# Weighted values with the head's values stationary and the turned probabilities moving, and the shares applied before the turn

## The reference, cut to what matters

```python
p = jax.nn.softmax(s, axis=-1)                       # first block, 8 heads
o = jnp.einsum('btngk,btknd->btngd', p, v_g)         # weighted values

p = jnp.exp(scores - m[..., None])                   # second block, kind 0
den = jnp.sum(p, axis=-1)
o = jnp.einsum('brnqhk,brnkhd->brnqhd', p, vb) / den[..., None]
ya = ya * jax.nn.silu(za)                            # the gate, per token and feature
pa = ya @ w_proj_a
```

## Time and profile before

| | |
|---|---|
| runs | 1718.6 us median of 3 (1718.58 to 1718.79) |
| the profiled execution's own time | 1716.0 us |
| its span, first to last instruction | 1714.1 us |
| TensorE busy | 1688.9 us, 13056 matmuls |
| VectorE busy | 1169.4 us |
| ScalarE busy | 941.9 us |
| GpSimd busy | 191.8 us |

### The profile page before, as it was taken

One profiled execution on the slowest core, in us unless ns is written; L12 is line 12 of the kernel. 1 busy time (PEld: TensorE's weight loads), 2 busy tenths in 40 slices (PEclk: granted clock), 3 DMA queues, 4 the chain that ended last, 5 costly groups with the idle time before them and its releaser, 6 DMA issues.

```text
span 1714.1 us, 30930 instructions
## 1 busy us (share of the span) xinstructions
PE 1688.9 (99%) x13056; PEld 1539.5 (90%) x13056; DVE 1169.4 (68%) x1631; ACT 941.9 (55%) x1386; POOL 191.8 (11%) x208
## 2 busy tenths in 40 slices
PE   7999999999999999999999999999999999999998
PEld 6989999999998989999999998888788988887887
DVE  7877555787877976547787875656765656567664
ACT  5584434654455574335554554665774546657742
POOL 0454500000001645200000000000000100000000
PEclk9999999999999999999999999999999999999999
DMA  6433523445444423424455545434345453344451
GB/s 227 170 133 106 182 103 124 172 174 195 173 170 170 173 99 131 161 100 153 168 196 183 179 182 177 148 124 172 133 156 188 163 200 145 126 169 148 150 194 49
DMA packets 48056, 268.33 MB, mean 157 GB/s; under 512 B 13552, under 2 KB 14448, under 8 KB 16176
## 3 DMA queue, kind: packets, MB, share of 16 engines
q1 hardware_dynamic: 38448, 264.80, 43.4%
q10 hardware_dynamic: 8704, 0.53, 0.3%
q0 software_dynamic: 768, 1.05, 0.3%
HBM read 264.52 MB, written 1.84 MB: 155 GB/s over the span
## 4 chain that ended last, share of the span: by engine, by line
PE 91%; DVE 5%; ACT 1%; POOL 1%; issue 0%; DMA 0%; SPq 0%; POOLq 0%; DVEq 0%; ACTq 0%
PE bank L1389 15%; PE bank L1390 14%; PE bank L1391 14%; PE bank L2484 10%; PE bank L2486 10%; PE bank L2485 10%; DVE w_low L905 2%; PE bank L2514 1%; PE bank L1626 1%; PE bank L1628 1%; PE bank L1627 1%; PE bank L2555 1%; PE bank L2502 1%; PE bank L1783 1%; DVE arena L1131 1%; ACT arena L632 1%
## 5 line engine op out<-in xcount | busy, mean ns | idle before, releaser
L905 DVE TENSOR_TENSOR w_low<-slab,w_high 128x2048 fp32r<-128x2048 f32 x250 | 585.8, 2348 | 237.3 <-ACT w_high L566 230.5
L1389 PE MATMUL bank<-act_high,w_high 128*128 128x256 f32 x2304 | 660.4, 287 | 0.1
L1390 PE MATMUL bank<-act_low,w_high 128*128 128x256 f32 x2304 | 651.8, 283 | 0.0
L1391 PE MATMUL bank<-act_high,w_low 128*128 128x256 f32 x2304 | 651.6, 283 | 0.0
L566 ACT ACTIVATE w_high<-slab 128x2048 fp32r<-128x2048 f32 x250 | 474.0, 1897 | 154.9 <-PE bank L2486 88.4
L1389 PEld LDWEIGHTS bank<-act_high,w_high 128*128 128x128 f32 x2304 | 441.7, 192 | 9.0 <-issue 6.1
L1390 PEld LDWEIGHTS bank<-act_low,w_high 128*128 128x128 f32 x2304 | 441.9, 192 | 1.1 <-issue 1.0
L1391 PEld LDWEIGHTS bank<-act_high,w_low 128*128 128x128 f32 x2304 | 441.8, 192 | 0.0
L2484 PE MATMUL bank<-w_high,act_high 128*128 128x512 f32 x768 | 305.8, 398 | 0.0
L2486 PE MATMUL bank<-w_low,act_high 128*128 128x512 f32 x768 | 300.7, 392 | 0.0
L2485 PE MATMUL bank<-w_high,act_low 128*128 128x512 f32 x768 | 299.9, 390 | 0.0
(11 more groups left out here) (240 smaller groups left out, 1732.6 us busy)
## 6 DMA issues: line engine op xcount, KB each, us to landing
slab<-stream_a SPq DMA_DIRECT2D x144, 1024.0 KB, 4.8
slab<-stream_b SPq DMA_DIRECT2D x104, 1024.0 KB, 4.7
residual<-x_t SPq DMA_DIRECT2D x4, 256.0 KB, 5.5
lora_weights<-lora SPq DMA_DIRECT2D x2, 512.0 KB, 8.0
out_t<-residual SPq DMA_DIRECT2D x4, 256.0 KB, 2.2
d_inverse<-arena POOLq DMA_DIRECT2D x2, 256.0 KB, 2.4
constants<-common SPq DMA_DIRECT2D x1, 384.0 KB, 9.6
constants_a<-const_a SPq DMA_DIRECT2D x1, 368.0 KB, 10.0
```

Source lines behind the costliest of these rows:

```text
L905: line.did(line.eng.tensor_tensor(core.wl[u % PARTS][:, 0:SLAB_WIDTH[u]], core.slab[u % SLABS][:, 0:SLAB_WIDTH[u]], core.wh[u % PARTS][:, ...
L1389: eng.matmul(out, wh, xh, start=first, stop=False, skip_group_check=True)
L1390: eng.matmul(out, wh, xl, start=False, stop=False, skip_group_check=True)
L1391: return eng.matmul(out, wl, xh, start=False, stop=last, skip_group_check=True)
```

## The change

The two operands of the weighted values change places. Now one head's values (128 keys x 64 features) are stationary and its turned probabilities move. For the first 128 keys both query blocks move in one product of 256 columns; for the second 128 keys only the second query block does, 128 columns. A pair takes four products instead of six, and the outputs have the features on the partitions: head 0 of the pair on partitions 0 to 63, head 1 on 64 to 127, 256 tokens in the columns. Since a token's denominator is then no longer a per-partition factor, the shares are applied before the turn: VectorE multiplies the exponentials by the reciprocals in place (`dve_share`: `share` in the a stages, `combine` for k < 8 in the b stages), and the turn waits for it (`shared`, `combined`) instead of for the exponentials.

In the a stages the output needs no transposes any more: pv on ScalarE and VectorE writes the high and low halves from bank 7 for each pair, and post is gone. In the b stages ScalarE copies bank 7 into the arena for each pair (VectorE's part of pv is gone), and the gate z is transposed instead of the gated output: z_turn(i) and y(i) behind the units (V, 2), (V, 3), (Q, 0), (Q, 1), and post(i), now from the arena, one unit later. The branch product in the a stages waits for one pair's halves at a time. The late turn goes from pair 0 of kind 0 to head 8, the first of kind 1.

```diff
+def dve_share(core, line, k, buf, tally):
+    rden = core.small[:, RDEN_:RDEN_ + 4]
+    line.settled()
+    line.did(line.eng.reciprocal(rden, core.small[:, DEN_ + 4 * (k % 4):][:, 0:4]))
+    line.settled()
+    for m in range(2):
+        part = buf[:, :, SPAN[m]]
+        line.did(line.eng.tensor_tensor(part, part, rden[:, 2 * m:2 * m + 2].unsqueeze(2).broadcast_to([P, 2, WIDTH[m]]), ALU.mult),
+                 tally if m else None)
+
+def pe_weighted(eng, out, p_t, value):
+    blocks = p_t.rearrange("p (n t) -> p n t", t=P)
+    for s in range(2):
+        for p in range(2):
+            o, v = out[HD * p:HD * p + HD], value(s, p)
+            if s == 0:
+                ins = eng.matmul(o[:, 0:T].rearrange("p (m t) -> p m t", m=2), v, blocks[:, p:2 * p + 3:2 + p], start=True, stop=False,
+                                 skip_group_check=True)
+            else:
+                ins = eng.matmul(o[:, P:T], v, blocks[:, 3 + 2 * p], start=False, stop=True, skip_group_check=True)
+    return ins
...
@@ schedule_a @@
-        work = [... (("pv", 3), ("turn", 2), ("scores", 0)) ...]
+        work = [... (("pv", 3), ("turn", 2), ("share", 1), ("scores", 0)) ...]
-    put(("ga", 1), ("invert", 0), ("tok", 1), ("post", 0), ("post", 1))
+    put(("ga", 1), ("invert", 0), ("tok", 1))
@@ schedule_b @@
-            late = (kind, n) == (0, 2)
+            late = (kind, n) == (1, 2)
-                put(UNITS_B[host + n], ("turn_late", 0))
+                put(UNITS_B[host + n], ("turn_late", 8))
-    put(("V", 3), ("y", 0), ("y", 1), ("y", 2), ("y", 3))
-    for i, unit in enumerate((("Q", 0), ("Q", 1), ("K", 0), ("K", 1))):
-        put(unit, ("post", i))
+    for i, unit in enumerate((("V", 2), ("V", 3), ("Q", 0), ("Q", 1), ("K", 0))):
+        if i < 4:
+            put(unit, ("z_turn", i), ("y", i))
+        if i:
+            put(unit, ("post", i - 1))
@@ a, ScalarE and VectorE: pv @@
+        act(core.xh[:, k, :], bank[7][:, 0:T], ACT.Copy, sem("ya_high"))
+        did(tt(core.xl[:, k, :], bank[7][:, 0:T], core.xh[:, k, :].bitcast(F32), ALU.subtract), sem("dve_emptied7"))
@@ b, ScalarE: pv, k < 8 @@
+            act(core.a(BO_ + k)[:, 0], bank[7][:, 0:T], ACT.Copy, sem("act_emptied7"))
@@ b, VectorE: pv gone; y and post, kind 0 @@
+            o = core.a(BO_ + 2 * i, 2)
+            did(tt(o, heads(bank[6 + i % 2], T), o, ALU.mult), sem(f"dve_emptied{6 + i % 2}"))
+            did(tt(low, core.a(BO_ + 2 * i, 2), high, ALU.subtract), sem("y_low"))
@@ b, TensorE: turn, pv, z_turn @@
+        sem("combined").at_least(eng, k + 1)
-            banks.fill(7, "dve")
+            banks.fill(7, "act")
+            ins = pe_weighted(eng, bank[7], p_t, lambda t, p: v[:, t, P * i + HD * p:P * i + HD * p + HD])
+    def z_turn(i):
+        if i == 0:
+            eng.wait_ge(*sem("z_ready").upto(1))
+        b = 6 + i % 2
+        banks.fill(b, "dve")
+        ... four transposes of by_token(core, BZ_[0], m), as post had of the output
```

More of the change, by code:

```diff
@@ L421, in schedule_a @@
         put(unit, *([("conv", n - 2)] if 2 <= n < 6 else []), *rwkv[n])
-        work = [(name, n - lag) for name, lag in (("pv", 3), ("turn", 2), ("scores", 0)) if 0 <= n - lag < 4]
+        work = [(name, n - lag) for name, lag in (("pv", 3), ("turn", 2), ("share", 1), ("scores", 0)) if 0 <= n - lag < 4]
         put(unit, *(work + [ROUND_NEXT] if unit == ("uc", 2) else [ROUND_NEXT] + work))
@@ L767, in turn, with pv @@
             act(turned_of(core, k, APT_)[:, at:at + n], bank[b][:, 0:n], ACT.Copy, sem(f"act_emptied{b}"))
-    def post(n):
-        eng.wait_ge(*sem("outputs_turned").next(eng))
-        act(core.xh[:, 2 * n:2 * n + 2, :], heads(bank[6 + n], T), ACT.Copy, sem("ya_high"))
+    def pv(k):
+        eng.wait_ge(*sem("weighted").upto(k + 1))
+        act(core.xh[:, k, :], bank[7][:, 0:T], ACT.Copy, sem("ya_high"))
     def lora_inputs(_):
@@ L1152, in scores, with share @@
         did(ts(mx, mx, -1.0, None, ALU.mult), sem("maxed"))
+    def share(k):
+        eng.wait_ge(*sem("exps").upto(k + 1))
+        dve_share(core, line, k, scores_of(core, k, ASC_), sem("shared"))
     def pv(k):
[L1155 to L1166, removed]
         eng.wait_ge(*sem("ya_high").next(eng))
-        did(tt(core.xl[:, 2 * n:2 * n + 2, :], heads(bank[b], T), core.xh[:, 2 * n:2 * n + 2, :].bitcast(F32), ALU.subtract),
-            sem(f"dve_emptied{b}"))
+        did(tt(core.xl[:, k, :], bank[7][:, 0:T], core.xh[:, k, :].bitcast(F32), ALU.subtract), sem("dve_emptied7"))
         line.tell(sem("ya_done"))
@@ L1564, in tile @@
         def tile(i, k):
-            if i == 0 and k % 2 == 0:
+            if i == 0 and name == "ya_done":
+                eng.wait_ge(*sem(name).upto(k + 1))
+            elif i == 0 and k % 2 == 0:
                 eng.wait_ge(*sem(name).upto(k // 2 + 1))
@@ L1684, in turn @@
         buf = scores_of(core, k, ASC_)
-        eng.wait_ge(*sem("exps").upto(k + 1))
+        eng.wait_ge(*sem("shared").upto(k + 1))
         for m, b in enumerate((6, 5)):
@@ L1697, in pv @@
         eng.wait_ge(sem("act_emptied5").sem, turn.at[k])
-        p_t = turned_of(core, k, APT_)
         banks.fill(7, "dve")
[L1700 to L1716, removed]
-                                    core.const("ident"))
-        ins.then_inc(sem("outputs_turned").sem, 1)
+        pe_weighted(eng, bank[7], turned_of(core, k, APT_),
+                    lambda t, p: half_of(core, WS_, t)[:, P + HD * p:P + HD * p + HD]).then_inc(sem("weighted").sem, 1)
     def lora(_):
@@ L2218, in post @@
         kind, i = n // 4, n % 4
-        eng.wait_ge(*sem("outputs_turned").next(eng))
         at = 8 * (1 - kind) + 2 * i
-        scale = core.small[:, LAM_ + 1:LAM_ + 2] if kind else 1.0
-        act(core.xh[:, at:at + 2, :], heads(bank[6 + i % 2], T), ACT.Copy, sem("y_high"), scale=scale)
+        if kind:
+            eng.wait_ge(*sem("outputs_turned").upto(n + 1))
+            act(core.xh[:, at:at + 2, :], heads(bank[6 + i % 2], T), ACT.Copy, sem("y_high"), scale=core.small[:, LAM_ + 1:LAM_ + 2])
+        else:
+            eng.wait_ge(*sem("outputs_gated").upto(n + 1))
+            act(core.xh[:, at:at + 2, :], core.a(BO_ + 2 * i, 2), ACT.Copy, sem("y_high"))
     def gate(g):
@@ L2354, in combine @@
     def combine(k):
+        eng.wait_ge(*sem("exps").upto(k + 1))
         if k < 8:
+            dve_share(core, line, k, scores_of(core, k, BSC_), sem("combined"))
             return
-        eng.wait_ge(*sem("exps").upto(k + 1))
         rden = shares(k)
@@ L2385, in y @@
         kind, i = n // 4, n % 4
+        if kind == 0:
+            eng.wait_ge(*sem("outputs_turned").upto(n + 1))
+            if n == 0:
+                eng.wait_ge(*sem("act_emptied7").upto(16))
+            o = core.a(BO_ + 2 * i, 2)
+            did(tt(o, heads(bank[6 + i % 2], T), o, ALU.mult), sem(f"dve_emptied{6 + i % 2}"))
+            line.tell(sem("outputs_gated"))
+            return
         if i == 0:
-            eng.wait_ge(*sem("z_ready").next(eng))
+            eng.wait_ge(*sem("z_ready").upto(2))
         if n == 4:
@@ L2409, in post @@
                     op1=ALU.subtract), sem(f"dve_emptied{b}"))
+            line.tell(sem("y_low"))
         else:
-            did(tt(low, heads(bank[b], T), high, ALU.subtract), sem(f"dve_emptied{b}"))
-        line.tell(sem("y_low"))
+            did(tt(low, core.a(BO_ + 2 * i, 2), high, ALU.subtract), sem("y_low"))
     def merge(i):
```

62 lines of the change are left out of this document (24 added, 38 removed).

## The result

The changed kernel takes 1728.1 us (median of 8 runs, 1723.6 to 1731.3), the kernel before 1718.6 (8 runs, 1716.5 to 1719.3): a ratio of 1.0055, 95% interval 1.0041 to 1.0068. That is 9.5 us slower, where 3.7 us faster was forecast and 1721.5 was the top of the range. The profiled execution took 1729.8 us for a span of 1728.0, at a mean granted clock of 0.987 of 2.4 GHz (before: 0.993).

A forecast was written before the change was run, and what follows sets the result against it. TensorE's own queue was taken as the bound, plus places where it waits for late engines. Terms of -2.1 (b steps and qk_turn), -0.7 (b turn order) and -0.9 (a stages) made -3.7 us, hence 1714.9 us, range 1711.3 to 1721.5.

The forecast's parts named there:

- The step: One weighted-value step on TensorE: 0.85 plus 0.09 to 0.19 us against 1.29, taken as 0.30 us saved.
- Rivals 3 and 4: Weighted-value step: 3, half overlap, saves nothing, 1718.6 us, chance 0.13; 4, no overlap, 1722.2 to 1723.8 us, chance 0.17.
- Waits of the b stages: b stages: TensorE waits for ScalarE's bank 7 copy in six places, 0.3 to 0.5 us each; such hosts lose 0.15.
- two new waits of 0.75: In each b stage TensorE waits 0.75 us for head 0's shares (`combined`) before its turn.
- none at head 8: b stages: with turn(8) put last, the 1.1 us wait before its transposes (L2524) is covered.
- The a stages' line: a stages: scores(1) and pair 1's maxima 2.2 to 3.2 us later, L1748 1.1 us late; net -0.9 us for both.
- a wait of TensorE elsewhere: Sign of being wrong: TensorE waits at places not named, such as the gate's transposes for `z_ready`.
- later than 103.68: a stages: GpSimd's L1949 comes later than 103.68 us, so ScalarE's square starts 0.6 to 1.6 us later.
- rival 2: a stages: full overlap, GpSimd and VectorE miss each other, 1.1 us back in each: 1712.0 us, chance 0.2.
- The 2 us to spare before the first chunk: a stages: after the attention part, the orders before the first chunk have over 2 us to spare.
- the transposes: a stages: the attention output's eight transposes go, 0.95 us net a stage, 1.9 us over two stages.

The follow-up runs named there:

- b_one_half: Against b_only, both heads' weighted-value products on the same column half, the second head's outputs left out: 1721.5 us, ratio 1.0026.
- b_only: Against the changed kernel, the a stages' programs and order of work put back as before, b stages as changed: 1715.6 us, ratio 0.9993.
- low_last: Against the changed kernel, VectorE's low half of the a stages' weighted values moved to the end of its host: 1725.2 us, ratio 1.0035.
- first_share_last: Against the changed kernel, only in the second host VectorE does scores(1) ahead of share(0): 1722.9 us, ratio 1.0021.
- mended: Against the changed kernel, a-stage scores ahead of the previous pair's shares, VectorE copy of bank 7, pair 2's turn last for both softmaxes: 1713.0 us, ratio 0.9981.
- a_no_share: Against the changed kernel, the a stages' shares (reciprocal and products) left out, hand-overs kept: 1716.2 us, ratio 0.9993.

## Why the prediction was wrong

- **The step.** Forecast 0.85 us or more with a cost of 0.09 to 0.19 for the change of form, so 0.30 saved; measured 0.81 us, a little under the 0.85 to 0.95 named, and 0.35 us saved a host. Right, at the upper edge of its bounds. b_one_half shows the cause, overlap. The Trainium skill ("TensorE: Matmul & The Clock Gate", packing small matmuls) would have a load overlap only where row groups differ; here all 128 rows are shared and 0.81 against 1.45 us says otherwise, as its table does, which has 2.38 times for three column tiles. Rivals 3 and 4 fall.
- **Waits of the b stages.** Forecast: hosts with a raw copy 0.15 longer, two new waits of 0.75, none at head 8. Measured: 0.16 longer (9.04 against 8.88), 0.65, none. For both stages -2.8 was forecast and -3.0 (0.3) measured at full clock. The waits for the ScalarE copy are 2.9 us, six of 0.5, where six of 0.3 to 0.5 were forecast; they eat what the larger saving brings.
- **The a stages' line: the step that failed.** It stood at -0.9 for both stages, with 1.1 us of lateness a stage, 1.8 at most, at L1748. Against b_only the changed a stages cost 7.6 us at full clock and 3.9 more through the clock (0.9910 to 0.9888). The prediction named a wait of TensorE elsewhere as a sign of being wrong: L1741, L1732 and L1828 are three. Five things were off.
  - The maxima of pair 1 came 4.2 us late (97.64 to 101.89), not 2.2 to 3.2. The delay by share(0) was foreseen, and is 2.8 us (scores(1) at 98.08 for 95.26), 1.7 of it collision. Not foreseen was that the delay carries the tiny negation behind it onto GpSimd's next operation, 1.4 us more. The trace of before had a sign of that, as the negation of pair 0 meets a GpSimd operation there:

```profile
91.64 1.29 POOL L1943 TENSOR_TENSOR arena<-arena 128x512 f32<-128x512 f32 x1
...
91.70 1.27 DVE L1152 TENSOR_SCALAR small<-small 128x4 f32<-128x4 f32 x1
```

  - GpSimd was forecast to be done with the keys later than 103.68, as before. It was early: the multiplication starts at 99.94 for 101.78, as its collision with the split went away (1.42 us for 3.09), which rival 2 had thought possible. It gave nothing back, since ScalarE now waited for the maxima.
  - The prediction followed this delay to L1691 and L1748 and not to bank 5, which passes from the copy of the turned probabilities to the sums of kk. That wait had no row before, since the copy came in time: 4.3 us in both stages.
  - VectorE's own wait for ScalarE's high half was in no term of the sum. pv was costed on ScalarE's queue alone; but what stands behind it on VectorE (a share, the scores) waits too. low_last measures it at 3.5 us.
  - The clock was taken as given. The three profiled kernels with waits of over 1.5 us at L1741 or L1732 (changed, low_last, first_share_last) have seven of them; five were followed within 2 us by 3 to 7 us at 1.2 GHz, two weren't (that at 617.19 above is one). Their mean clocks are 0.9888, 0.9881 and 0.9886 against 0.9907 to 0.9917 in the other sets of the changed forms, with standard errors of 0.0003 to 0.0009. A stretch of lower clock at 128 to 136 us comes in b_only's profile too, with no such wait, so single dips prove nothing; the means do show the difference. What decides whether a wait is followed by one stays open.
- **The 2 us to spare before the first chunk, and the transposes.** The 2 us aren't there: L1828 waits 1.5 us a stage for the inverses even in mended. The shares aren't the cause, as a_no_share waits 1.45 and 1.42 us there. Nor was there room before: TensorE came to this product 43.7 us after the last product of the chunks (159.91 to 203.65, start to start) without a wait, and in a_no_share, without the eight transposes between, it is there after 43.0 us and the inverses after 44.45 (161.75, 206.20). So most of the 1.9 us booked for the transposes turned into waiting here. Why the inverses also land later was not separated.

## What to carry to other kernels

Where work is put ahead of the link that others wait for, follow that link through every bank and every queue it feeds until the slack is used, including hand-overs that show no wait yet; and look at what tiny instruction lands beside a long GpSimd operation. When waits of a few kernels are compared, take the span times the granted clock beside the median. A regrouping of matmuls can be right and be lost by where its helpers stand: kept out of the a stages, with one copy on another engine and one more turn put last, the kernel is 0.6% faster than before (8.1 us at full clock, 2.4 of them from the turn order alone).

## What the runs showed of the hardware

- Products of 128 rows by 64 columns on the two column halves of TensorE run side by side in fp32, 0.81 against 1.45 us for eight records, in either order of the program.
- A VectorE tensor_scalar on 128x4 elements took 0.17 us alone, 0.30 to 0.65 in part and 1.74 us in full collision with a GpSimd tensor op of 1.90 us. The Trainium skill ("SBUF — State Buffer", on the shared port pair) names the lock; the trace agrees: the op of 1.74 us ends at 101.86, GpSimd's at 101.84, and the one of 1.27 us at 92.97, GpSimd's at 92.93. So the price was what the GpSimd operation had left, however small the VectorE op.
- Five of seven waits of TensorE of 1.55 to 2.19 us in the attention hosts were followed by 3 to 7 us at 1.2 GHz; of eleven waits of 1.39 to 2.01 us at L1828 only the longest was. On the mean of the runs the lower clock cost nearly as much as the waits (4.3 and 4.6 us).
